# Weights and early modulation weights laid out by the host: one run of 8 KB per partition for each 1 MB transfer

## What is computed

```python
for i in range(DEPTH):                       # DEPTH = 2
    mod_lat = (silu_c @ ada_w[i] + ada_b[i])  # ada_w[i]: 2048 x 12288
    sh1, sc1, g1, sh2, sc2, g2 = jnp.split(mod_lat, N_MOD, axis=-1)
    h_lat = modulate(rms_norm(x, norm_mix_g[i]), sh1, sc1)
    if mixer == 0:                            # layer 0
        q_l, k_l, v_l = project_qkv(h_lat, attn_w_qkv[j], attn_q_norm_g[j], attn_k_norm_g[j])
        k_c, v_c = project_kv(h_ctx, attn_w_qkv[j][:, D_MODEL:], attn_k_norm_g[j])
        o_lat = latent_attention(q_l, k_l, v_l, k_c, v_c) @ attn_w_o[j]
    else:                                     # layer 1
        o_lat = fourier_mix(h_lat, fourier_w_o[j])
    x = x + g1 * o_lat
    x = x + g2 * sq_relu_mlp(modulate(rms_norm(x, norm_mlp_g[i]), sh2, sc2), mlp_w1[i], mlp_w2[i])
return rms_norm(x, final_norm_g)
```

## Time and profile before

| | us |
|---|---|
| median of 3 runs | 2005.79 |
| lowest, highest | 2003.09, 2006.72 |
| the profiled execution, its time | 2005.52 |
| its span, first to last instruction | 2003.6 |
| TensorE busy in it | 1965.9 (98%) |
| VectorE busy | 1391.5 (69%) |
| ScalarE busy | 969.3 (48%) |

### The profile page before, as it was taken

How to read it: one execution, slowest core, us unless ns; L and a number is a source line. 1 busy time by engine, 2 the same in 40 slices (tenths; PEclk the granted TensorE clock), 3 DMA queues, 4 the chain that set the end, 5 groups by cost and what they waited for, 6 DMA issues and landing times.

```text
span 2003.6 us, 24992 instructions
## 1 busy us (share of the span) xinstructions
PE 1965.9 (98%) x10188; PEld 1609.5 (80%) x10188; DVE 1391.5 (69%) x1424; ACT 969.3 (48%) x1265; POOL 110.9 (6%) x196
## 2 busy tenths in 40 slices
PE   6999989999999999999999999999999999999998
PEld 4677756778888888888888888788888888888886
DVE  3666998889867787788888675766666455555556
ACT  6432565455544455544444464555554454444444
POOL 1111001000000000000000000000000000000000
PEclk9999999999999999999999999999999999999999
DMA  9998768779989899799999626577776566555653
GB/s 359 338 378 319 277 257 297 272 252 323 353 293 348 313 360 364 262 367 363 355 395 383 219 85 193 175 252 253 257 251 220 187 192 210 189 192 198 218 190 126
DMA packets 152261, 542.80 MB, mean 271 GB/s; under 512 B 9393, under 2 KB 10577, under 8 KB 114641
## 3 DMA queue, kind: packets, MB, share of 16 engines
q1 hardware_dynamic: 119312, 335.77, 47.9%
q0 software_dynamic: 31744, 201.34, 27.1%
q10 hardware_dynamic: 1090, 4.09, 0.5%
HBM read 535.91 MB, written 2.10 MB: 269 GB/s over the span
## 4 chain that ended last, share of the span: by engine, by line
PE 94%; DVE 3%; ACT 1%; DMA 1%; issue 1%; POOL 0%; ACTq 0%; DVEq 0%; POOLq 0%
PE ps L2098 13%; PE ps L2036 12%; PE ps L2032 12%; PE ps L2035 11%; PE ps L2096 11%; PE ps L2099 6%; PE ps L1848 6%; PE ps L2095 6%; PE ps L1849 5%; PE ps L1850 5%; PE ps L2257 1%; PE ps L1913 1%; PE ps L2204 1%; DMA spare<-in_ada_w 1%; PE ps L2242 1%
## 5 line engine op out<-in xcount | busy, mean ns | idle before, releaser
L1201 DVE TENSOR_TENSOR w_lo<-raw,w_hi 128x1024 fp32r<-128x1024 f32 x616 | 749.5, 1223 | 467.9 <-ACT w_hi L727 467.6
L727 ACT ACTIVATE w_hi<-raw 128x1024 fp32r<-128x1024 f32 x616 | 649.4, 1059 | 845.7 <-PE ps L2036 345.8
L2098 PE MATMUL ps<-hh,w_hi 128*128 128x512 f32 x1088 | 427.5, 398 | 1.1 <-DVE hh L1627 1.1
L2032 PE MATMUL ps<-w_hi,hh 128*128 128x512 f32 x992 | 385.9, 389 | 0.0
L2036 PE MATMUL ps<-w_hi,hh 128*128 128x512 f32 x992 | 385.9, 389 | 0.0
L2035 PE MATMUL ps<-w_lo,hh 128*128 128x512 f32 x992 | 385.9, 389 | 0.0
L2096 PE MATMUL ps<-hh,w_hi 128*128 128x512 f32 x960 | 379.9, 396 | 0.0
L2099 PE MATMUL ps<-hh,w_lo 128*128 128x256 f32 x1088 | 302.9, 278 | 0.0
L2095 PE MATMUL ps<-hh,w_lo 128*128 128x256 f32 x960 | 267.5, 279 | 0.0
L2099 PEld LDWEIGHTS ps<-hh,w_lo 128*128 128x128 f32 x1088 | 205.7, 189 | 40.9
L2035 PEld LDWEIGHTS ps<-w_lo,hh 128*128 128x128 f32 x992 | 186.2, 188 | 38.9
(11 more groups left out here) (252 smaller groups left out, 1620.4 us busy)
## 6 DMA issues: line engine op xcount, KB each, us to landing
raw<-in_mlp_w SPq DMA_DIRECT2D x256, 1024.0 KB, 5.3
ada_raw<-in_ada_w POOLq DMA_DIRECT2D x151, 1024.0 KB, 6.2
spare<-in_ada_w POOLq DMA_DIRECT2D x29, 1024.0 KB, 6.6
raw<-in_attn_w_qkv SPq DMA_DIRECT2D x24, 1024.0 KB, 10.1
raw<-in_attn_w_o SPq DMA_DIRECT2D x16, 1024.0 KB, 5.7
raw<-in_fourier_w_o SPq DMA_DIRECT2D x16, 1024.0 KB, 5.1
g_row<-in_ada_w POOLq DMA_DIRECT2D x12, 1024.0 KB, 9.0
g_row<-gate_rows SPq DMA_DIRECT2D x48, 64.0 KB, 5.2
```

The costliest lines, as they stand in the source:

```text
L727: act.activation(w_slot(s)[0], raw[:, piece % RAW, s % 2, :], ACT.Copy).then_inc(hi_ready, 1)
L1201: nc.vector.tensor_tensor(lo, raw[:, s // 2 % RAW, s % 2, :], hi.bitcast(F32), ALU.subtract).then_inc(lo_ready, 1)
L2032: ins = mm(bank_of(tt, nb), h_hi[:, k % KT, tok], hi[:, cols], start=start, stop=False)
L2098: mm(both, w_hi[:, s % SPLIT, w], hh[:, k, :, :], start=(k == 0), stop=False, skip_group_check=True)
```

## The change

The host, before the launch, permutes the weights into arrays in which each 1 MB piece is one block of 128 rows of 2048 floats. The same goes for the part of `ada_w[0]` that the 32 `load_start` pieces read, which is put into an extra array `start_ada_w` of 32 MB. The kernel's transfers then name one run of 8 KB per partition on both sides. What lands in each buffer is the same as before, in the same order and at the same place in every queue; the waits are the same. The down projection, the 160 `load_vector` pieces, x, the context rows and the small vectors are untouched.

```diff
-        def load_columns(piece, src):
-
-            if piece >= RAW:
-                sp.wait_ge(lo_ready, 2 * (piece - RAW) + 2)
-            dst = raw[:, piece % RAW, :, :].rearrange("p h (k n) -> p (h k) n", k=2)
-            sp.dma_start(dst, src).then_inc(raw_in[piece % RAW], 16)
-
-        def load_first(piece):
...
+        def load_packed(piece, src):
+
+            load_piece(piece, src.rearrange("p (h n) -> p h n", h=2))
...
         for p in range(24):
-            if p < 6:
-                load_first(p)
-            else:
-                load_columns(p, wqkv_v[p // 6, column_block(p)])
+            load_packed(p, w_qkv[p])
...
-                load_columns(P_WO[0] + 4 * b + q, wo_v[b, q])
+                load_packed(P_WO[0] + 4 * b + q, w_o[b, q])
...
-                        load_columns(P_WO[1] + 4 * b + q, wf_v[b, q])
+                        load_packed(P_WO[1] + 4 * b + q, fourier_w[b, q])
...
-                    load_columns(P_UP[l] + 4 * b + q, w1_v[l][b, q])
+                    load_packed(P_UP[l] + 4 * b + q, w1[l, b, q])
...
-            if n < 8:
-                dst, src = ring(start_slot(n)).rearrange("p (k c) -> p k c", k=8), first_v[n // 4, n % 4 // 2, n % 2]
-            else:
-                dst, src = ring(start_slot(n)).rearrange("p (k c) -> p k c", k=4), start_v[n // 8, n % 8 // 4, n % 4]
-            pool.dma_start(dst, src).then_inc(ada_in[start_slot(n)], 16)
+            pool.dma_start(ring(start_slot(n)), ada_start[n]).then_inc(ada_in[start_slot(n)], 16)
...
+def by_columns(w):
+
+    return w.reshape(4, 4, P, -1, 512).transpose(3, 0, 2, 1, 4).reshape(-1, 4, P, D)
...
+def start_pieces(w):
+
+    rows = w[:, 0:2 * D]
+    first = rows.reshape(2, 8, P, 2, 8, 2 * P).transpose(4, 3, 0, 2, 1, 5)[0:2].reshape(8, P, D)
+    later = rows.reshape(4, 4, P, 2, 4, 512).transpose(4, 3, 0, 2, 1, 5)[1:4].reshape(24, P, D)
+    return np.ascontiguousarray(np.concatenate([first, later]))
```

More of the change, by code:

```diff
@@ L245, in layer_block @@
 def layer_block(nc, x, c, ctx_in, c_ctx, ada_w, ada_b, norm_mix_g, norm_mlp_g, w_qkv, q_g, k_g, w_o,
-                fourier_w, w1, w2, final_g, ident_in, rope_in, dft_in, out):
+                fourier_w, w1, w2, final_g, ident_in, rope_in, dft_in, ada_start, out):
     stack = ExitStack()
@@ L480, in layer_block @@
     out_done = sem("out_done")
[L483 to L490, removed]
     w2_v = [w2[l].rearrange("(k p) (h n) -> k p h n", p=P, h=2) for l in range(2)]
@@ L555, in load_piece @@
             sp.dma_start(raw[:, piece % RAW, :, :], src).then_inc(raw_in[piece % RAW], 16)
-        def load_columns(piece, src):
-            if piece >= RAW:
-                sp.wait_ge(lo_ready, 2 * (piece - RAW) + 2)
-            dst = raw[:, piece % RAW, :, :].rearrange("p h (k n) -> p (h k) n", k=2)
-            sp.dma_start(dst, src).then_inc(raw_in[piece % RAW], 16)
-        def load_first(piece):
-            if piece >= RAW:
-                sp.wait_ge(lo_ready, 2 * (piece - RAW) + 2)
-            sp.dma_start(raw[:, piece % RAW, :, :], wqkv_first[piece // 3, piece % 3]).then_inc(raw_in[piece % RAW], 16)
+        def load_packed(piece, src):
+            load_piece(piece, src.rearrange("p (h n) -> p h n", h=2))
         def load_bias(v):
@@ L2427, with qkv_pieces @@
         "attn_k_norm_g", "attn_w_o", "fourier_w_o", "mlp_w1", "mlp_w2", "final_norm_g"]
+def by_columns(w):
+    return w.reshape(4, 4, P, -1, 512).transpose(3, 0, 2, 1, 4).reshape(-1, 4, P, D)
+def qkv_pieces(w):
+    first = w.reshape(8, 2, P, 3, NC).transpose(0, 3, 2, 1, 4)[0:2].reshape(6, P, D)
+    columns = by_columns(w)
+    return np.concatenate([first, np.stack([columns[column_block(p), p // 6] for p in range(6, 24)])])
+def start_pieces(w):
[3 more added lines that the diff above has]
+    return np.ascontiguousarray(np.concatenate([first, later]))
 def kernel(**inputs):
@@ L2444 @@
             a = a[:, TOKENS]
+        if name == "attn_w_qkv":
+            a = qkv_pieces(a[0])
+        if name in ("attn_w_o", "fourier_w_o"):
+            a = by_columns(a[0])
+        if name == "mlp_w1":
+            a = _np.stack([by_columns(a[0]), by_columns(a[1])])
         a = _np.ascontiguousarray(a)
@@ L2450 @@
         args.append(nc.dram_tensor(f"const_{name}", a.shape, _mybir.dt.from_np(a.dtype), kind="ExternalInput").ap())
+    arrays["start_ada_w"] = start_pieces(inputs["ada_w"][0])
+    args.append(nc.dram_tensor("start_ada_w", (32, P, D), _mybir.dt.float32, kind="ExternalInput").ap())
     args.append(nc.dram_tensor("out_0", (1, T, D), _mybir.dt.float32, kind="ExternalOutput").ap())
```

## The result

| | before | after |
|---|---|---|
| median of 18 runs each, us | 2005.77 | 2009.93 |
| lowest to highest | 2003.09 to 2007.70 | 2007.55 to 2012.41 |
| ratio, 95% interval | | 1.0021 (1.0015 to 1.0027) |
| span of the profiled execution | 2003.6 | 2005.8 |

The kernel became 4.2 us slower. The forecast was 2008.0 with 2002.8 to 2011.0 as its range. The measured 2009.93 is in it, in the part over 2009.8 to which the prediction gave a chance of 0.15.

What follows compares the result with a forecast made beforehand. The prediction took TensorE, nearly always busy, to bound the kernel, with the path to its first product open to change. Later x added 2.5 us to 2005.5, other terms counted nothing: 2008.0, range 2002.8 to 2011.0.

Steps and rivals of the forecast that it cites:

- What bounds the kernel: Whole kernel: TensorE busy 1965.9 of 2003.6 us, so at most 38 us to gain, hardly anywhere but the beginning.
- The two ways that end nearly together: Before the first product: x's transposes end at 22.68, piece 3 comes at 22.97; the later way sets the end.
- The pieces move faster: Beginning: a 1 MB `ada_w` piece takes 2.5 us instead of 3.0; gain at most 0.3 us.
- They start sooner, and x comes later: Beginning: POOL's data starts at about 2.5 us, x comes 2.8 us late (0.9 to 3.4), path 2.5 us longer.
- SP's loads: cost nothing: Beginning: SP's first `raw`, waiting for piece 1, is not late; cost nothing, covered by the 6.3 us chain.
- The clock: TensorE's lower-clock stretch from 30 to 40 us, costing 1.7 us, counted at nothing, with 1.7 to both sides.
- The steady part: Up projection: `raw` lands 0.5 us sooner, `ada_w` 0.7 later; TensorE waits for neither, cost and gain nothing.
- The third rival: Attention stretch: later `ada_w` rows hold up VectorE, its DMA waits in 220 to 440 us exceeding 4; 2012 us, chance 0.10.
- The first rival: Beginning: POOL's first data still comes at 5.5 us, x 0.9 late; +0.6, 2006.1 us, chance 0.22.
- the second: Beginning: x is not delayed at all; path gains 0.3, perhaps 1.7 more from the clock; 2005.2 to 2003.5 us, chance 0.18.
- the fourth: All changed transfers: packets stay as they were because engines cut runs their own way; 2005.5 us, chance 0.05.
- The sum: Whole kernel: 2005.5 us for the profiled execution plus 2.5 from the longer path at the beginning gives 2008.0.

Runs made afterwards that it cites:

- both waits in place: POOL waits for the first half of x and SP waits for piece 2: 2004.85 us in the kernel after, 2006.61 in the kernel before.

## Why the prediction was right, and where not

**What bounds the kernel: right.** By the medians the end moved 4.2 us and the first product 3.9. From 100 to 150 and from 700 to 1140 us TensorE is as full as before.

**The two ways that end nearly together: misread.** The prediction puts the start of the transposes of x at 20.71 down to x, which VectorE had finished at 20.15. But there was no wait for x before them: TensorE came straight from piece 2, for which it had waited 0.27 us. By the rows of the run with the small vectors on SP they can start 0.8 us after VectorE begins on the second half, so in the kernel before at 18.73 + 0.81 = 19.5. x had 1.2 us to spare (20.71 less 19.5), which the step "the transposes start at 20.71 + 2.8" doesn't have.

**The pieces move faster: right.** 422 GB/s against 349 from 10 to 20 us, and no gain from it, since x and the small vectors behind it were the later way. With both waits in place there was a gain of 1.8 us.

**They start sooner, and x comes later: right, and the size was a little low.** I had x 2.8 us late with 3.4 as the upper end; it was 3.45. It was the equal share that I took (1.07 MB and 1.07 MB), but x also began worse than an equal share: 0.30 MB against 0.64 by 5.5 us. That POOL's pieces beside x are the cause is shown by the run in which POOL waits: x is there at 9.32. It doesn't separate the earlier start from the longer packets, since neither stands beside the first half of x there. An estimate from the rows by queue does: 0.57 MB less by 5.5 us (0.87 less 0.30), at the 1.07 MB in 5.1 us that x then gets, are 2.7 us; the 0.18 MB less in the next 5.1 us (1.25 less 1.07) are 0.9. So the earlier start is the larger part. The prediction's reason for it, the 1024 runs that have to be written down, isn't shown: issued at 7.15, the same transfers had their first data within 1.9 us.

**A term that was left out.** The four small vectors stand behind x in the same queue, and TensorE's order needs them before piece 2 and the transposes. I didn't count them. In the kernel after x alone would have allowed the transposes at 23.0; the small vectors held them to 25.43. That is 2.4 us, as much as x itself costs (20.71 to 23.0, 2.3 us). Moving them to SP took the wait away and pushed x by 1.1 us.

**"SP's loads: cost nothing": wrong as a step.** I looked only at whether `raw` itself would be late. With packed weights and old early pieces the kernel lost 2.1 us: piece 3 came 1.2 us later. In the kernel after, the small vectors are later than with the early pieces alone packed, by 1.2 us (22.76 against 21.52). The step should have asked who else is on the engines when SP's longer packets come.

**The clock: within its range.** The stretch at the lower clock after 30 us was absent in both profiles of the kernel after (granted clock 1.00 from 30 to 40) and there in both of the kernel before (0.83), so in the profiled execution the kernel after is spared the 1.7 us, and TensorE is busy 1.8 us less. Piece 3 took 1.07 us in place of 1.52, but this isn't that stretch: the table has the granted clock at 1.00 from 22 to 30 us in both kernels and so doesn't show why, and in the second profile of the kernel before piece 3 took 1.12. The mean clock of a run differs from execution to execution (0.997 and 0.999 for the kernel after), so I don't credit the change with a gain in the median.

**The steady part: right in the sum, and `ada_w` the other way.** Landing times in 440 to 700 us, then 930 to 1140 us, in the kernel after:

```profile
raw<-in_mlp_w SPq DMA_DIRECT2D x45, 1024.0 KB, 6.5
ada_raw<-in_ada_w POOLq DMA_DIRECT2D x33, 1024.0 KB, 5.2
...
raw<-in_mlp_w SPq DMA_DIRECT2D x39, 1024.0 KB, 6.2
ada_raw<-in_ada_w POOLq DMA_DIRECT2D x29, 1024.0 KB, 6.2
```

`raw` gained 0.4 us against the earlier trace rows, where I had 0.5. `ada_w` didn't lose 0.7, it gained 0.4. VectorE's waits for it grew all the same, from 2.6 us to 8.4 in the same stretch:

```profile
DVE ada_sum L1204 <- DMA ada_raw<-in_ada_w: 8.4, 5, 3.4
```

TensorE didn't notice (440.00 of 440.00 from 700 to 1140 us, 258.57 of 260.00 from 440 to 700, where it was 258.58 before). The third rival, that VectorE's waits in the attention stretch exceed 4 us, is out: there is no wait for DMA among them in 220 to 440 us. The first rival is out by the 0.64 MB before 5.5 us, the second by x at 14.81, the fourth by the packets.

**The sum.** The transposes start 4.7 us later: 2.3 from x (3.45 us later, less the 1.2 that it had to spare) and 2.4 from the small vectors. Piece 3 then follows 0.4 us sooner behind them, with its wait of 0.28 gone, and the way from piece 3 to the first product is 0.5 us shorter (5.85 against 6.32). That makes 3.9, as measured. The runs say 4.2.

So the sign and the mechanism were right: POOL's pieces start sooner and take engine time from x. That the size came within 1.7 us is partly luck. With 1.2 us to spare, the prediction's own 2.8 us for x would have moved the transposes by 1.6 us and not by 2.8. The small vectors, which it put at nothing by not naming them, cost 2.4 us and happened to make up for it.

## What to carry to other kernels

Before a transfer is made faster, look at which transfers it runs beside, and which of them is needed first: all queues draw on the same 16 engines, and a queue that starts sooner can take its share from one whose data is needed first. Here, with the old layout, POOL's queue moved nothing for the first 5.5 us, and this had given x a head start by accident. Packed, the kernel was slower than before as it stood, and faster once one wait put that head start back on purpose. Then look at what stands behind the delayed transfer in its queue, and at what the waiting engine does in the order of its program: the end of a transfer is on the path only if the engine waits for it there. When the first microseconds are the subject, compare the place of the first product in several profiles and not the spans, since the clock can move these by as much.

## What the runs showed of the hardware that I had not expected

The time from POOL's issue to the first data of its queue isn't fixed by the number of runs. With 128 runs of 8 KB it was 1.2 us (issue at 99.22, kernel before), 1.4 (1.25, kernel after) and 1.8 (6.91, POOL waits for half of x). With 1024 runs of 1 KB it was 4.3 us at the start of the kernel before (1.26), about 3.7 later in it (32.17), 1.7 in the kernel with the early pieces as before (31.87), and 1.8 in the kernel before with POOL held back (7.15). POOL's issue itself went from 890 to 527 ns on the median.

Two executions of one program differ in how long TensorE's clock is at its lower level: mean clock 0.997 and 0.999 for the kernel after, 0.996 and 0.995 for the kernel before. At 2005 us each 0.001 is 4 us more at that level and 2 us of span, so the steps from 0.995 to 0.997 among the 18 runs of the kernel after are about as large as their spread of 5 us.

A small transfer behind a large one in the same queue was late by more than the large one. x was used 3.45 us later in the kernel after. The last of the small vectors, which are 128 KB in all, landed 22.7 us after the start in place of 15.3, so 7.5 us later.
